# Key matrices transposed by VectorE in 32x32 blocks inside the levels, instead of by TensorE

## What is computed

```python
z = h @ w_in                       # [r | k | v | g | u | g_pool | gate_a | gate_b]
kk = normalize(kf * k_k)           # per head
kf = kf * (1.0 + (a - 1.0) * k_a)
# per token and head, S is [value, key]:
sa = S @ a_t                       # a_t = -kk
S  = S * w_t + outer(sa, b_t) + outer(v_t, k_t)    # b_t = kk * a
o  = S @ r_t
```

## Time and profile before

| | us |
|---|---|
| median of 3 runs (1281.93 to 1283.6) | 1283.43 |
| profiled execution | 1280.37 |
| its span, first to last instruction | 1278.8 |
| TensorE busy | 1239.0 |
| VectorE busy | 722.1 |
| ScalarE busy | 544.2 |
| GpSimd busy | 219.1 |

### The profile page before, as it was taken

One profiled execution on the slowest core, in us unless ns is written; L12 is line 12 of the kernel. 1 busy time (PEld: TensorE's weight loads), 2 busy tenths in 40 slices (PEclk: granted clock), 3 DMA queues, 4 the chain that ended last, 5 costly groups with the idle time before them and its releaser, 6 DMA issues.

```text
span 1278.8 us, 22437 instructions
## 1 busy us (share of the span) xinstructions
PE 1239.0 (97%) x8460; PEld 1191.5 (93%) x8460; DVE 722.1 (56%) x1028; ACT 544.2 (43%) x870; POOL 219.1 (17%) x299
## 2 busy tenths in 40 slices
PE   4999999999999999999999899999999999999996
PEld 4889999999999999999999799999999999979996
DVE  6866475756647575664758754444444444465441
ACT  5263453727345372734536233333333343344341
POOL 2241130403113040311207200000000400001111
PEclk9999999999999999999999899999999999999998
DMA  9614323332432333243145444545455874424550
GB/s 224 197 34 111 108 62 114 85 98 75 110 108 62 115 85 98 75 110 108 50 117 151 137 128 137 164 135 160 138 157 144 233 208 133 143 72 135 165 152 24
DMA packets 274138, 155.50 MB, mean 122 GB/s; under 512 B 6949, under 2 KB 269773, under 8 KB 273444
## 3 DMA queue, kind: packets, MB, share of 16 engines
q1 hardware_dynamic: 266896, 137.03, 38.2%
q0 software_dynamic: 7056, 17.91, 5.5%
q10 hardware_dynamic: 148, 0.04, 0.0%
HBM read 149.57 MB, written 5.61 MB: 121 GB/s over the span
## 4 chain that ended last, share of the span: by engine, by line
PE 91%; DVE 5%; ACT 1%; issue 1%; DMA 1%; SPq 0%; POOL 0%; POOLq 0%; DVEq 0%; ACTq 0%
PE acc L1453 18%; PE acc L1454 17%; PE acc L1455 17%; PE wide L1455 5%; PE wide L1454 5%; PE wide L1453 5%; PE wide L1472 3%; PE wide L1624 3%; PE wide L1617 2%; DVE wl L1003 1%; PE wide L1542 1%; PE wide L1832 1%; PE wide L1630 1%; PE wide L1584 1%; DVE win_a L1280 1%
## 5 line engine op out<-in xcount | busy, mean ns | idle before, releaser
L1003 DVE TENSOR_TENSOR wl<-wraw,wh 128x1024 fp32r<-128x1024 f32 x256 | 319.8, 1255 | 220.3 <-ACT wh L666 218.2
L666 ACT CAST wh<-wraw 128x1024 fp32r<-128x1024 f32 x256 | 267.5, 1047 | 296.2 <-PE acc L1455 199.0
L1453 PE MATMUL acc<-hh,wh 128*128 128x320 f32 (+1 forms) x1084 | 365.5, 337 | 7.1 <-DVE wl L1003 7.1
L1454 PE MATMUL acc<-hl,wh 128*128 128x320 f32 (+1 forms) x1084 | 337.8, 312 | 0.0
L1455 PE MATMUL acc<-hh,wl 128*128 128x320 f32 (+1 forms) x1084 | 337.3, 311 | 0.0
L1453 PEld LDWEIGHTS acc<-hh,wh 128*128 128x128 f32 x1084 | 205.8, 190 | 11.3 <-issue 7.8
L1454 PEld LDWEIGHTS acc<-hl,wh 128*128 128x128 f32 x1084 | 205.7, 190 | 3.4
L1455 PEld LDWEIGHTS acc<-hh,wl 128*128 128x128 f32 x1084 | 205.0, 189 | 0.0
L1453 PE MATMUL acc<-x1h,wh 128*128 128x320 f32 x256 | 82.5, 322 | 0.4 <-DVE x1l L1410 0.4
L1453 PE MATMUL acc<-mh,wh 128*128 128x320 f32 x256 | 80.6, 315 | 0.0
L1455 PE MATMUL acc<-x1h,wl 128*128 128x320 f32 x256 | 79.1, 309 | 0.0
(11 more groups left out here) (351 smaller groups left out, 2267.6 us busy)
## 6 DMA issues: line engine op xcount, KB each, us to landing
wraw<-in_w_in SPq DMA_DIRECT2D x160, 512.0 KB, 3.8
wraw<-in_w_branch SPq DMA_DIRECT2D x32, 512.0 KB, 4.0
wraw<-in_w_out SPq DMA_DIRECT2D x32, 512.0 KB, 4.0
wraw<-in_w_ple_gate SPq DMA_DIRECT2D x32, 512.0 KB, 3.9
xt<-in_x_prompt SPq DMA_DIRECT2D x2, 1024.0 KB, 7.0
S0n<-in_state_wkv POOLq DMA_DIRECT2D x16, 128.0 KB, 6.3
out<-so POOLq DMA_DIRECT2D x16, 128.0 KB, 3.0
xt<-in_x_prompt POOLq DMA_DIRECT2D x2, 1024.0 KB, 7.3
```

The source lines that it names most:

```text
L666: A.copy(wh[:, slot, :], wraw[:, slot, :]).then_inc(s["hi_ready"], 1)
L1003: V.tensor_tensor(wl[:, slot, :], wraw[:, slot, :], wh[:, slot, :].bitcast(F32), ALU.subtract).then_inc(s["lo_ready"], 1)
L1453: M.matmul(out[:, 0:width], wh[:, slot, wcol], hi, start=first, stop=False)
L1454: M.matmul(out[:, 0:width], wh[:, slot, wcol], lo, start=False, stop=False)
```

## The change

The ten transposes on TensorE and the two copies on ScalarE go. In each level VectorE runs four transposes of its own, of 32 partitions and GP x 32 = 128 elements, straight from bU (or kBD) to the place of the block in BtBD (or KtBD); sixteen make both tiles for a pair. Only the 4 chunks of the prompt are turned, and the tiles shrink to [128, GP, 2, 64]. The off-diagonal blocks must be zero, so GpSimd clears both tiles with the others. The stream steps keep their number: 3 + 3 behind scores and the first transposes become 6 behind scores.

```diff
@@ GpSimd
-            blocks = (vBD, aBD, bBD, kBD, YBD, ZaBD, EndBD)
+            blocks = (vBD, aBD, bBD, kBD, YBD, ZaBD, EndBD, BtBD, KtBD)
@@ ScalarE, mix
-                act.wait_ge(s["bt_ps"], r + 1)
-                A.copy(BtBD[:, :, :, :].rearrange("p g h c -> p (g h c)"), B45[:, 0:2 * T])
-
-                act.wait_ge(s["kt_ps"], r + 1)
-                A.copy(KtBD[:, :, :, :].rearrange("p g h c -> p (g h c)"), B23[:, 0:2 * T])
@@ VectorE, mix
+                def turned_keys(first, last):
+                    for n in range(first, last):
+                        of_k, h, kb, cb = n // 8, n // 4 % 2, n // 2 % 2, n % 2
+                        rows, cols = slice(HD * h + BLK * kb, HD * h + BLK * (kb + 1)), slice(BLK * cb, BLK * (cb + 1))
+                        src = kBD[rows, 0:GP, h, cols] if of_k else grp(bU)[rows, 0:GP, cols]
+                        V.transpose((BtBD, KtBD)[of_k][HD * h + BLK * cb:HD * h + BLK * (cb + 1), :, h, BLK * kb:BLK * (kb + 1)],
+                                    src).then_inc(s["key_turned"], 1)
+
@@ VectorE, level n
                     turned(n)
                     if n:
                         go(3 + n)
+                    turned_keys(4 * n, 4 * n + 4)
                     dve.wait_ge(s["t_ps"], r * (LEVELS + ROUNDS) + (ROUNDS + n + 1))
@@ VectorE, before the pairs
+            dve.wait_ge(s["filled"], 3 + 9)
@@ TensorE, mix
-            AFTER = dict(maps=13, key_norm=6, values=4, bonus=9, scores=3, keys=3, product=3,
+            AFTER = dict(maps=13, key_norm=6, values=4, bonus=9, scores=6, product=3,
...
                 pe.wait_ge(s["ark_ready"], r + 1)
-                for g in range(G):
-                    last = transpose(B45[:, P * g:P * (g + 1)], flat(bBD, g))
-                last.then_inc(s["bt_ps"], 1)
-                st.advance(AFTER["keys"])
-                for g in range(G):
-                    last = transpose(B23[:, P * g:P * (g + 1)], flat(kBD, g))
-                last.then_inc(s["kt_ps"], 1)
@@ TensorE, chain over the chunks
+                    if g == 0:
+                        pe.wait_ge(s["key_turned"], r * 16 + 16)
                     M.matmul(B[0][:, 0:C], flat(KtBD, g), Vs[:, g, :], start=True, stop=False)
```

More of the change, by code:

```diff
@@ L42 @@
 C = 64
+BLK = 32
 G = T // C
@@ L236, in build @@
         YBD = r1.take("YBD", [P, G, 2, C])
-        BtBD = r1.take("BtBD", [P, G, 2, C])
-        KtBD = r1.take("KtBD", [P, G, 2, C])
+        BtBD = r1.take("BtBD", [P, GP, 2, C])
+        KtBD = r1.take("KtBD", [P, GP, 2, C])
         VtBD = r1.take("VtBD", [P, G, 2, C])
@@ L278, in build @@
         O_s, dO, dsq, sd = cl, pd, pi, kf
+        r1.next += 2 * 2 * C
         uS = r1.take("uS", [P, 8, T])
@@ L355, in build @@
             s0t_ready ksq_ready decay_in kk_max kk_norm cum_ready cumx_ready ah_ready bh_ready z_ps zabd_ready vt_ps
-            vs_ready bt_ps y_ready ybd_ready x_ready kt_ps tail_ps s_ready sd_ready endbd_ready
+            vs_ready y_ready ybd_ready x_ready key_turned tail_ps s_ready sd_ready endbd_ready
             sbd_ready ubd_ready end_ps o_ps o_ready send_ps dev_ready dsq_ready var_ps sd_done y_done yah_ready gsil_ready
@@ L1270, in window @@
                 samples = ues[g][:, :, BUF + TP:E].rearrange("p k (b t) -> p k b t", b=NB)
-                dve.wait_ge(s["filled"], 13 + 2 * g + 2)
+                dve.wait_ge(s["filled"], 15 + 2 * g + 2)
                 a = NB * BUF * (2 * g % 4)
```

## The result

| | before | after |
|---|---|---|
| median, 4 runs each | 1282.97 us | 1316.84 us (1313.57 to 1322.07) |
| profiled execution | 1280.37 us | 1316.23 us |
| its span | 1278.8 us | 1314.7 us |
| ratio, 95% interval | | 1.0269 (1.0234 to 1.0303) |

The change makes the kernel 34 us slower, 2.7%. The forecast was 1309 us (+25.9) in a range of 1295 to 1326. Direction and range hold; 8 us are missing from the sum.

What follows compares the result with a forecast made beforehand. TensorE, busy for 97% of the span, bounds the kernel, its update in levels 1 to 3 waiting for VectorE's Tm. Terms 35.0 + 0.9 - 10.0 = +25.9 us on the median 1283.43 give 1309 us, range 1295 to 1326.

Steps and rivals of the forecast that it cites:

- transposes in levels: Four VectorE transposes ahead of Tm in each level delay TensorE's update: 4.38 us a pair, 35.0 us for eight.
- What bounds, and where the slack isn't: TensorE bounds; in levels 1 to 3 its update already waits 0.13 us for VectorE's Tm, whose queue has no slack.
- Price of a transpose: On VectorE, 305 ns for each 32x128 transpose, step 0.335 us, 1.34 us for four, from a line through two shapes.
- Level 0: First level, without a split: 0.98 us of cover against 1.34 us of transposes, so 0.36 us shows.
- Removed work: TensorE's transposes of bBD (0.71 us) and kBD (0.54 us) go: 1.25 us a pair, 10.0 us for eight.
- Fills on GpSimd: Two further fills, run once, delay cur_m and ScalarE ahead of the first pair's zr: 0.9 us, between 0 and 1.0.
- Rival (c): Stands of some 1.5 us in each level halve TensorE's clock there: +100 us, 1400 us; chance 3%.
- Rival (a): VectorE's idle 1.27 us in each level takes in the transposes, so only removed work less fills counts: 1274 us; 4%.

Runs made afterwards that it cites:

- e3: Kernel before with the sixteen VectorE transposes added ahead of Tm, TensorE's transposes and ScalarE's copies kept: 1325.9 against 1282.09 us.
- e8: Changed kernel with each level's four transposes behind Tm and the two fills on VectorE instead of GpSimd: 1274.17 against 1281.71 us.
- e1: Changed kernel with each level's four transposes moved behind Tm, all else the same: 1276.8 against 1282.09 us for the kernel before.
- e5: Kernel before with only the two further fills on GpSimd, ScalarE waiting for them once: 1287.26 against 1281.71 us.
- e10: Changed kernel, four transposes still ahead of Tm, with the two fills on VectorE: 1320.2 against 1282.03 us for the kernel before.
- e4: Changed kernel with BtBD and KtBD at their old size, so no tile moves: 1320.04 us, ratio 1.0291 to the kernel before.
- e9: Changed kernel with the transposes spread over VectorE's idle times and the two fills on VectorE: 1270.59 against 1282.03 us for the kernel before.
- e7: Changed kernel with 7 transposes behind the score masks and 2, 3, 3, 1 behind Tm: 1276.6 against 1281.71 us for the kernel before.
- e2: Changed kernel without the sixteen transposes and TensorE's wait for them, states computed from zeros: 1274.37 against 1282.09 us for the kernel before.
- e6: Changed kernel with two transposes ahead of Tm in each level instead of four, KtBD empty: 1293.66 against 1281.71 us for the kernel before.

## Why the prediction was right, and by how much it was off

Against the profiled execution (35.9 us more in the span):

| step | forecast, 8 pairs | measured | from |
|---|---|---|---|
| transposes in levels | +35.0 | +37.9 | e3, 8 x 4.74 |
| removed from TensorE | -10.0 | -9.8 | e8, 8 x 1.23 |
| fills, first pair | +0.9 | +1.05 | products with zr start at 95.96 instead of 94.91 us |
| fills, the other pairs | 0 | +1.8 | starts of pairs 1 to 6 in after against e8's 21.77 |
| falling clock, and tail | 0 | the rest, +4.9 | 1.6 in pair 0; 3.3 behind the last pair |

- **What bounds, and where the slack isn't: right.** The levels ran on VectorE's queue up to Tm, with 0.13 us of waiting and no slack. After beside e1 shows it: the same instructions in the same level, on one or the other side of one wait and of Tm, 40 us apart.
- **Price of a transpose: right.** 0.335 us apiece was taken from the line through two shapes; the rows show durations of 0.303 and 0.302 us and 1.31 us for four with the gap behind them. The rule that instructions have a fixed part (the Trainium skill, "VectorE: DVE Perf Modes", The TRN2 errata) fits: a quarter of 64x256's work per instruction (half the partitions, half the columns) costs 69% of its time.
- **Level 0: a term that was too small.** 0.36 us forecast, 0.49 measured; levels 1 and 3 cost 1.46 where 1.34 was put, level 2 1.32. The split and Tm used to overlap by 0.08 us. In levels 1 and 3 the transposes don't start until 0.03 us after the split, in level 2 they overlap with it as Tm did. Together 0.36 us a pair, 2.9 us.
- **Removed work: right in size (1.25 us, e8: 1.23).** In the changed kernel only 0.86 us of it is seen, because of the next point.
- **Fills on GpSimd: the step that failed in kind.** They were costed as a delay of the first pair. That is there, but they also moved GpSimd's start against VectorE's in later pairs, which none of the rows before shows. e5 has it without any of the rest, and e8 and e10, with the fills on VectorE, don't have it.
- **Rival (c), the clock: dismissed on a row that shows nothing.** The row of 20 to 25 us gives a clock of 1.00 at a lower busy share, and from it stands of 1.5 us in 5.6 were called safe. But the trace of the kernel before has no record of the clock ahead of 28.5 us, and the row gives 1.00 where there is none. TensorE's passes from 26.0 to 27.9 us start 0.27 us apart, as those at 706 to 710 us do with the clock at 0.50, so they run at the lower level; from 28.79 us on the step is 0.15 us. In the changed kernel, whose record begins sooner, the same stretch has falls:

```profile
26.55 0.47 PE L1524 MATMUL acc<-hl,wh 128*128 128x328 f32 x1
26.82 0.47 PE L1523 MATMUL acc<-hh,wh 128*128 128x328 f32 x1
...
28.79 0.31 PE L1453 MATMUL acc<-hh,wh 128*128 128x328 f32 x1
28.94 0.31 PE L1454 MATMUL acc<-hl,wh 128*128 128x328 f32 x1
```

```profile
20.00:25.00 5.00, 1.85 (x18) 1.23 (x16) 4.93 (x12) 3.36 (x4) 2.98 (x4) 0.84 1.13 282
25.00:30.00 5.00, 4.53 (x16) 4.54 (x17) 5.00 (x5) 4.31 (x5) 2.50 (x5) 0.50 1.05 214
```

  The loss wasn't 100 us, since the clock falls for 3.4 or 6.8 us at a time and the levels take part of it in. It cost 1.6 us in the profile of after (its pair 0 takes 80.59 us, that of e4, without a fall, 79.01) and 9.4 us in that of e10. The chance was put at 3% for a large loss; a small loss with a large chance was no case at all. That the large one stayed away isn't the merit of the row.
- **Rival (a), idle time takes the transposes in:** wrong as the change was written, and right as soon as they stand behind Tm (e1) or are spread (e9). The 10.0 us of the sum were there to be had; e9 gives 11.4, with an interval of 8.5 to 13.2.
- **The tail: 3.3 us of the 35.9, not shown to come from the change.** Behind the pairs a wait of TensorE for ytmp was 3.0 us at its longest, where it was 1.6. The same longer wait (2.8 to 3.0) is in e3 to e8 and in e10, and e5, e7 and e8 have no stands in the levels; it is 1.6 in e1 and 1.8 to 1.9 in e2 and e9. From the last pair's final product on VectorE (yf) to the end the profiles take 602.1 us (before) to 605.3 us (after, e7). What sets it is open; a difference of up to 3 us between two profiles can be this alone.
- **Sum and range.** The 8 us that the forecast lacks are 2.9 in the levels, 0.2 of removed work, 0.2 and 1.8 of the fills, and 4.9 of clock and tail, together 10.0 in the profiled execution; the medians are 2.0 us closer. The upper bound comes out at 1326.7 us, which the prediction gives once as 1326 and once as 1327. The levels and the removed work, which carry the forecast, were right without luck; that the clock stayed a small term was luck.

## What to carry to other kernels

Before work is given to an engine that is busy for half of the time, find in its queue the instruction that the bottleneck waits for. Ahead of it every microsecond beyond the slack counts in full; behind it, as far as the idle time up to the next wait reaches, it is nearly free. Here one moved line was worth 40 us. When TensorE is the bottleneck, a recurring stand can cost more than its length, since the clock may fall behind it; that fall is paid only where TensorE isn't about to stand again. Even an instruction that runs once can shift how two engines meet in a loop. And before a row of the clock is used as evidence, check the step from pass to pass beside it.

## What the runs showed of the hardware

- GpSimd and VectorE slow each other down when some of their instructions run at once, and which of them pays hangs on the lead of one, with the border at 0.15 us: kf 1.22 and scan 0.81 us in one order, 0.61 and 1.12 us in the other.
- The granted clock falls to 0.50 behind stands of TensorE of 1.5 us that recur each 5.6 us, in one to seven of eight pairs; with stands of 0.8 us in 4.9 (e6) it didn't fall in any pair. A fall of 3.4 us costs 1.4 to 1.6 us where TensorE is busy without a gap, and nothing where a stand of 1.5 us follows it.
- VectorE's transposes of 32x128 f32 take 0.30 us and don't overlap: seven in a row took 2.29 us in e9.
